# Prompt attention on one core: the order of transposes, scores and value products on TensorE

## What is computed

```python
def nsa_attend(q, gates, qpos, ctx, k_w, v_w, kpos_w):
    k_c, v_c, c_end, overlap, k_blk, v_blk = ctx
    s_c = jnp.einsum('bqghd,bcgd->bqghc', qg, k_c) * scale          # compressed blocks
    p_c = jax.nn.softmax(jnp.where(valid_c, s_c, NEG), axis=-1) * valid_c
    o_c = jnp.einsum('bqghc,bcgd->bqghd', p_c, v_c)
...
    s_s = jnp.einsum('bqghd,bgqskd->bqghsk', qg, k_s) * scale       # selected blocks
    p_s = jax.nn.softmax(jnp.where(valid_k, s_s, NEG), axis=-1)
    o_s = jnp.einsum('bqghn,bgqnd->bqghd', p_s, v_s)
    s_w = jnp.einsum('bqghd,bkgd->bqghk', qg, k_w) * scale          # sliding window
    p_w = jax.nn.softmax(jnp.where(valid_w, s_w, NEG), axis=-1)
    o_w = jnp.einsum('bqghk,bkgd->bqghd', p_w, v_w)
    o = g[..., 0:1] * o_c + g[..., 1:2] * o_s + g[..., 2:3] * o_w
```

## Time and profile before

| what | value |
|---|---|
| time, median of 3 runs | 3099.03 us (3095.54 to 3099.3) |
| the profiled execution | 3066.72 us, span 3065.3 us |
| PE / DVE / ACT / POOL busy, share of the span | 94% / 45% / 25% / 7% |
| mean granted PE clock (1.00 is 2.4 GHz) | 0.964 |
| the prompt's attention loop | 184 us, 6% of the span |

### The profile page before, as it was taken

One profiled execution on the slowest core, in us unless ns is written; L12 is line 12 of the kernel. 1 busy time (PEld: TensorE's weight loads), 2 busy tenths in 40 slices (PEclk: granted clock), 3 DMA queues, 4 the chain that ended last, 5 costly groups with the idle time before them and its releaser, 6 DMA issues.

```text
span 3065.3 us, 52634 instructions
## 1 busy us (share of the span) xinstructions
PE 2881.5 (94%) x21290; PEld 2658.6 (87%) x21290; DVE 1376.0 (45%) x2015; ACT 759.4 (25%) x1163; POOL 218.5 (7%) x323
## 2 busy tenths in 40 slices
PE   7999999898989799999998999999979968999999
PEld 7999998686868599999977899999955546999999
DVE  4434433535353654244531443445468744543342
ACT  3211222222222222122212221223135512321121
POOL 0000003212121000000003000000010031000000
PEclk9999999999999899999999999999879978999999
DMA  3222232333333322222336122222140064222222
GB/s 106 82 87 76 89 110 75 110 118 120 108 132 102 117 76 93 79 82 94 115 110 184 55 88 84 82 91 76 49 145 1 1 199 124 69 82 89 76 87 88
DMA packets 81327, 287.59 MB, mean 94 GB/s; under 512 B 10464, under 2 KB 18720, under 8 KB 80560
## 3 DMA queue, kind: packets, MB, share of 16 engines
q1 hardware_dynamic: 60192, 205.02, 21.0%
q0 software_dynamic: 21008, 80.76, 7.8%
HBM read 260.97 MB, written 33.16 MB: 96 GB/s over the span
## 4 chain that ended last, share of the span: by engine, by line
PE 85%; DVE 7%; DMA 2%; issue 2%; ACT 2%; POOL 1%; POOLq 0%; ACTq 0%; SPq 0%; DVEq 0%
PE ps L420 69%; PE ps L635 4%; DVE att_stats L1680 1%; PE ps L1246 1%; DMA sample_state<-in_state 1%; DVE probs L1692 1%; PE ps L1225 1%; PE ps L1582 1%; PE ps L684 1%; ACT w_high L302 1%; DMA out_state_s<-sample_state 1%; PE ps L1811 1%; PE ps L1463 1%; DVE probs_T L1702 1%; PE ps L1096 1%
## 5 line engine op out<-in xcount | busy, mean ns | idle before, releaser
L307 DVE TENSOR_TENSOR w_low<-w_staged,w_high 128x1024 fp32r<-128x1024 f32 (+1 forms) x334 | 441.0, 1320 | 554.9 <-ACT w_high L302 554.0
L302 ACT ACTIVATE w_high<-w_staged 128x1024 fp32r<-128x1024 f32 (+1 forms) x334 | 372.5, 1115 | 1074.3 <-PE ps L420 931.2
L420 PE MATMUL ps<-xh_f,w_high 128*128 128x288 f32 x2816 | 605.8, 296 | 31.8 <-DVE xl_f L400 23.7
L420 PE MATMUL ps<-xl_f,w_high 128*128 128x288 f32 x2816 | 603.5, 295 | 0.0
L420 PE MATMUL ps<-xh_f,w_low 128*128 128x288 f32 x2816 | 603.3, 295 | 0.0
L420 PEld LDWEIGHTS ps<-xh_f,w_high 128*128 128x128 f32 x2816 | 452.8, 189 | 35.2 <-issue 27.5
L420 PEld LDWEIGHTS ps<-xh_f,w_low 128*128 128x128 f32 x2816 | 452.8, 189 | 0.0
L420 PEld LDWEIGHTS ps<-xl_f,w_high 128*128 128x128 f32 x2816 | 452.8, 189 | 0.0
L420 PE MATMUL ps<-hh,w_high 128*128 128x288 f32 x1408 | 300.2, 294 | 0.0
L420 PE MATMUL ps<-hl,w_high 128*128 128x288 f32 x1408 | 300.1, 294 | 0.0
L420 PE MATMUL ps<-hh,w_low 128*128 128x288 f32 x1408 | 300.1, 294 | 0.0
(11 more groups left out here) (367 smaller groups left out, 3748.4 us busy)
## 6 DMA issues: line engine op xcount, KB each, us to landing
w_staged<-in_wa SPq DMA_DIRECT2D x270, 512.0 KB, 3.5
w_staged<-in_wb SPq DMA_DIRECT2D x64, 704.0 KB, 4.0
sample_state<-in_state POOLq DMA_DIRECT2D x32, 512.0 KB, 5.7
out_state_s<-sample_state POOLq DMA_DIRECT2D x32, 512.0 KB, 4.3
cmp_pages<-in_pages_cmp POOLq DMA_DIRECT2D x64, 256.0 KB, 3.2
k_pages<-in_pages_k SPq DMA_DIRECT2D x32, 128.0 KB, 3.0
v_pages<-in_pages_v POOLq DMA_DIRECT2D x32, 128.0 KB, 3.2
q_T<-in_pages_k SPq DMA_DIRECT2D x32, 128.0 KB, 2.9
```

The source lines that it names most:

```text
L302: act.activation(wh[:, slot, 0:size], wf[:, slot, 0:size], ACT.Copy).then_inc(hi_ready, 1)
L307: dve.tensor_tensor(wl[:, slot, 0:size], wf[:, slot, 0:size], wh[:, slot, 0:size].bitcast(F32), ALU.subtract).then_inc(lo_ready, 1)
L420: mm = pe.matmul(ps[:, out + h, 0:HALF], w[:, slot, cols:cols + P], m[:, h * HALF:(h + 1) * HALF], start=(first and n == 0), stop=(last an ...
```

## The change

In PE's loop over the steps one call changes its place: turned(n) stands in front of scores(n + 2), where it stood behind. Nothing else is changed.

```diff
             pe.wait_ge(c_ta, 1)
             pe.wait_ge(vcr_ready, 1)
             for n in range(N_ATT):
+                turned(n)
                 if n + 2 < N_ATT:
                     scores(n + 2)
-                turned(n)
                 if n:
                     values(n - 1)
             values(N_ATT - 1)
```

## The result

The changed kernel takes 3256.0 us (median of 5 runs, 3251.3 to 3272.5), the kernel before 3095.5 us in the same comparison: a ratio of 1.054, with a 95% interval of 1.050 to 1.058. It is **160 us slower**. 105 us were forecast, and 3226 us was the end of the range: the sign and the place were right, the size was not.

A forecast was written before the change was run, and what follows sets the result against it. PE bounds the kernel; in the attention loop PE and DVE hold each other up in turn. 89 us of serial delay plus 16 us of lower clock, 105 us on the 3099 us median, gave 3204 us; range 3177 to 3226.

The forecast's parts named there:

- The ring: Prompt attention loop: scaling, transposes, scores, maxima, copy, next scaling run serially; 34.6 us a tile for 23.1, 89 us more.
- 4.2 + 1.4 + 9.7 + 0.3 = 15.6 us a tile: Attention loop, per tile: transposes' weight loads 4.2, steps to the scores 1.4, scores with mask 9.7, DVE-to-PE hand-over 0.3 us.
- The clock: PE's granted clock in the attention loop: mean between 1.00 and 0.77 because of PE's gaps, taken as 16 us more.
- the prediction's own formula: Attention loop: 13.9 us a tile of transposes and scores, stretched by the lower clock, over 7.75 tiles; 32 us at 0.77.
- Halving the 32 us: Attention loop: 16 us of the 32 at clock 0.77, as wide steps' gaps resemble a 1.87 us one, narrow steps' the old.
- The clock held at 1.00: Rival, attention loop: only the serial delay of 89 us at full clock, 3188 us; chance 0.20.
- The clock lost throughout: Rival, attention loop: clock stays at 0.50, transposes and scores double, 108 us on top, 3296 us; chance 0.06.
- The order doesn't matter: Rival, attention loop: PE's and DVE's idle time takes up the delay, 3099 us; chance 0.04.
- Not slower: Rival, attention loop: transposes come sooner, DVE's copies stop waiting, worth 10.1 us at most, 3089 us; chance 0.03.
- The signs: Expected in the new profile: loop about 289 us, 36 us a tile, DVE's waits for scores 100 us or more.
- The cover of the value products: Attention loop: value products, some 1.7 us at the widest, lie beside 3.07 us of DVE work and so cost nothing.

The follow-up runs named there:

- e1: The changed kernel with 53 pairs a tile of extra matmuls that add zero, ahead of the value products: 3180.9 us against 3095.1 before, ratio 1.029.
- e6: The changed kernel with DVE's maxima moved last, after copy and scaling: 3123.9 us, ratio 1.009 to the kernel before.
- e5: The kernel before, old order on PE, with DVE's maxima moved last, after copy and scaling: 3126.4 us, ratio 1.009.
- e4: The changed kernel with scores made three steps ahead in place of two: 3092.4 us, ratio 0.9998 to the kernel before.
- e8: The changed kernel with 13 pairs a tile of extra matmuls that add zero, ahead of the value products: 3212.3 us, ratio 1.036.

## Why the prediction was right and wrong

**The ring** was right, in place and size. It says that DVE comes to wait for the scores in every step: 62 of 62. It sums a tile to 34.6 us: 35.0 in e1, where the clock is held at 1.00. What DVE waits for in it was summed to 4.2 + 1.4 + 9.7 + 0.3 = 15.6 us a tile, and in e1 DVE waits 114.7 / 7.75 = 14.8 us a tile for the scores, so the parts fit and not only the total. It makes the cost 89 us: 86 by the medians of e1. That the ring needs the maxima first in DVE's queue, and is not a price of PE's order by itself, is shown by e6, with the new order at the time of e5, and by e4.

**The clock** was the step that failed, "So the new loop's mean clock lies between 1.00 and 0.77 [...] I take half, 16 us". It measured 74 us, by DVE's waits of the changed kernel and e1, and 75 by their medians. Two things were wrong in it, the first far larger.

First, 0.77 was no bound. The sample tokens' attention keeps PE busy 73% of its time; the ring was forecast to keep it busy 61%, so the loop could well lie beyond that row. The mean in the loop is 0.63, and with it the prediction's own formula gives 13.9 x (1/0.63 - 1) x 7.75 = 63 us. Halving the 32 us failed too. It rested on the narrow steps, whose gaps were to be like those of the old loop, but they are not spared: the narrow transposes at 2392.27 us, for one, run at 0.50.

Second, the mean over all time is not quite the clock of the ring's pieces. Their lengths grew 1.65 to 1.67 times, as if at a clock of 0.60, and 13.9 x 0.65 x 7.75 is 70 us, which leaves 4 of the 74.

The Trainium skill, page "TensorE: Matmul & The Clock Gate", section "A second HAM failure mode: psum-queue depth-cycling", tells of such a swinging clock, and this trace agrees, 0.50 and 1.00 in turn with a mean of 0.65 in a tile. The warning of the Trainium skill, same page, section "Why this matters for your kernels", is of longer gaps than the waits of 2.8 us at most seen here, and the clock fell all the same.

**The rivals.** The clock held at 1.00, 3188 us, is not what happened, but e1 makes that kernel, at 3181 us. The clock lost throughout, 3296 us, was not reached: it comes back in every tile. *The order doesn't matter* and *Not slower* fell with the 62 waits: the transposes do come out sooner, and DVE's wait for them fell by 6.9 us, against 176 us more for the scores.

**The signs.** PE's waits for DVE's scaling were to be some 90 us in nearly all steps: 80.9 us in 54. DVE's and ACT's busy time stayed. A tile was to take 36 us: 44.4. The loop's clock was to be 0.8 to 0.95: 0.63. The cover of the value products did not hold in every step. In the tile above, where they run at the lower clock ahead of a narrow step, the scaling ends at 2391.86 us and PE starts the transposes only at 2392.27:

```profile
2390.37 1.98 PE L1606 MATMUL ps<-probs_T,v_tok 128*64 128x128 f32 x16
2391.38 0.48 DVE L1692 TENSOR_SCALAR probs<-probs,att_gates 128x128 f32<-128x128 f32 x2
2392.27 0.69 PE L1582 MATMUL ps<-mats,probs 128*128 128x128 f32 x2
```

That is some 0.4 us in one step of the eight; L1706 waits for ACT as before, 4.3 us for 4.1.

## What to carry to other kernels

Moving a piece of work behind a wait costs that piece on every turn if the engine that wants it next has it first in its queue; look at the other engine's order before moving work on the one. Before a clock is taken from another stretch as a bound, compare how busy PE is there and how busy it will be in the new loop; here the row taken was the busier one. If a serial ring can't be opened, filling PE's gap may be worth more than it costs: here 53 pairs of useless matmuls a tile gained 75 us, and 24 gained nearly as much.

## What the runs showed of the hardware

In the changed loop the clock fell during or just after gaps of PE of 1.4 to 2.5 us (in the tile from 2368 us) and at times stayed down through whole steps. It stayed at 1.00 in the old loop, whose longest wait of PE for DVE was 1.2 us. The length of a gap does not decide it alone: in the changed loop it fell after a gap of 1.38 us, and in e8 it stayed at 1.00 for 30 us through gaps of up to 2.02 us.

```profile
2397.86:2428.58 30.72, 21.78 (x208) 14.74 (x208) 16.72 (x50) 11.65 (x37) 0.00 (x0) 1.00 0.00 1
```

```profile
2402.29 0.88 PE L1583 MATMUL ps<-mats,probs 128*128 128x128 f32 x6 [2.02 <-DVE probs L1697]
```

What else decides it the runs don't separate. With extra matmuls in the gaps the mean went from 0.63 to 0.82, 0.98 and 0.99. At the lower clock the step from the transposes to the scores took 0.33 us in place of 0.17, and over the loop 18.5 us in place of 10.4, which was counted as fixed.

The SwiGLU blocks of 3072 matmuls took either 399.6 or 409.9 us in these profiles (the first of the program 411 to 413), at a granted clock of 1.00 for either. What decides that was not looked into.
